# A quarter of the expert tables leaves the gathers: 4,096 of 16,384 experts computed densely on TensorE in a product-key expert FFN

## The reference, cut to what matters

```python
q  = (ht @ w_q).reshape(T, 8, 2, 128)            # 8 heads, two half queries
v1, i1 = top_k(q[:, :, 0] . sub_k1, 16)          # 128 sub keys each
v2, i2 = top_k(q[:, :, 1] . sub_k2, 16)
sc, ci = top_k(v1[..., :, None] + v2[..., None, :], 16)
eidx = e1 * 128 + e2                             # e1, e2: the sub keys; 16384 experts
gate = softmax(sc)
a    = einsum('cd,chkd->chk', h, u_emb[eidx])    # 8 * 16 experts for each token
out  = einsum('chk,chkd->cd', gate * gelu(a), v_emb[eidx])
hs   = rms_norm(hs + out)                        # meta tokens dropped
```

## Time and profile before

| | us |
|---|---|
| median of 3 runs (2062.25 to 2065.85) | 2062.91 |
| the profiled execution | 2061.19 |
| its span on the core | 2059.4 |
| PE busy in the span | 1281.3 |
| DVE busy | 1206.6 |
| POOL busy | 730.3 |
| ACT busy | 410.8 |
| moved by DMA | 686.92 MB, 334 GB/s mean |

### The profile page before, as it was taken

How to read it: one execution, slowest core, us unless ns; L and a number is a source line. 1 busy time by engine, 2 the same in 40 slices (tenths; PEclk the granted TensorE clock), 3 DMA queues, 4 the chain that set the end, 5 groups by cost and what they waited for, 6 DMA issues and landing times.

```text
span 2059.4 us, 21129 instructions
## 1 busy us (share of the span) xinstructions
PE 1281.3 (62%) x7844; PEld 774.2 (38%) x7844; DVE 1206.6 (59%) x2252; ACT 410.8 (20%) x808; POOL 730.3 (35%) x712
## 2 busy tenths in 40 slices
...
GB/s 184 167 172 184 162 200 210 217 190 234 184 184 271 211 353 278 381 421 421 411 421 421 407 421 421 422 421 422 422 421 422 422 422 421 422 421 421 422 408 327
DMA packets 116645, 686.92 MB, mean 334 GB/s; under 512 B 13120, under 2 KB 13120, under 8 KB 42048
## 3 DMA queue, kind: packets, MB, share of 16 engines
q0 software_dynamic: 96768, 589.34, 75.6%
q1 hardware_dynamic: 19792, 96.46, 13.5%
...
## 4 chain that ended last, share of the span: by engine, by line
DMA 49%; PE 34%; DVE 9%; issue 4%; POOL 2%; ACT 1%; DVEq 0%; POOLq 0%; ACTq 0%; SPq 0%
DMA uv<-v_tab,eidT 32%; DMA uv<-u_tab,eid 15%; DVE uv L1473 5%; PE ps L1933 5%; PE ps L1597 4%; PE ps L1514 2%; PE ps L1515 2%; PE ps L1516 2%; PE ps L1602 2%; DMA parts<-W 2%; PE ps L1604 2%; PE ps L1603 2%; POOL uv L538 2%; PE ps L1806 1%; PE ps L1808 1%
## 5 line engine op out<-in xcount | busy, mean ns | idle before, releaser
L1933 PE MATMUL ps<-uv,over_mL 128*32 128x512 f32 x2048 | 459.1, 990 | 726.6 <-DMA uv<-v_tab,eidT 609.7
L1473 DVE CUSTOM_DVE_ANT_0 uv<-uv,xn 128x2048 f32<-128x2048 f32 x256 | 586.3, 2292 | 485.1 <-DMA uv<-u_tab,eid 484.2
L1933 PEld LDWEIGHTS ps<-uv,over_mL 128*32 128x32 f32 x2048 | 51.1, 136 | 1109.9 <-DMA uv<-v_tab,eidT 969.1
L529 POOL DMA_INDIRECT uv<-u_tab,eid x256 | 265.8, 1038 | 567.4 <-DVE av L1473 417.9
L538 POOL DMA_INDIRECT uv<-v_tab,eidT x256 | 285.7, 1116 | 314.1 <-PE ps L1933 295.1
L867 ACT ACTIVATE ga<-av,st 128x16 f32<-128x16 f32 x16 | 4.9, 308 | 724.0 <-DVE av L1473 724.0
L943 DVE TENSOR_TENSOR low_ring<-ring,wh 128x2048 fp32r<-128x2048 f32 x43 | 101.1, 2353 | 74.7 <-ACT wh L569 74.6
L1602 PE MATMUL ps<-hH,parts 128*128 128x256 f32 x400 | 123.8, 309 | 2.0 <-DMA parts<-W 2.0
L501 POOL DMA_DIRECT2D parts<-W x80 | 70.1, 876 | 153.1 <-ACT parts L687 124.6
L1597 PE MATMUL ps<-xn,ring 128*128 128x256 f32 x480 | 113.1, 386 | 0.2
L1895 PE MATMUL ps<-h2T,ring 128*128 128x256 f32 x416 | 112.7, 434 | 0.0
...
## 6 DMA issues: line engine op xcount, KB each, us to landing
...
parts<-W POOLq DMA_DIRECT2D x160, 320.0 KB, 5.5
...
uv<-u_tab,eid POOLq DMA_INDIRECT x256, 17.3
uv<-v_tab,eidT POOLq DMA_INDIRECT x256, 17.6
...
```

The source lines that it names most:

```text
L529: pool.indirect_dma_start(uv[:, m % UV, 0, :], None, u_tab, bass.IndirectOffsetOnAxis(ap=eid[:, p, i:i + 1], axis=0)).then_inc(s_u[m % UV] ...
L1473: nc.vector.tensor_tensor_reduce(uv[:, m % UV, 0, :], uv[:, m % UV, 0, :], xn[:, T, :], 1.0, 0.0, ALU.mult, ALU.add, av[:, p % 2, i:i + 1] ...
L1933: ins = nc.tensor.matmul(ps[32 * n:32 * n + 32, 4 * T + j, :], zd[:, p % 2, 32 * r:32 * r + 32], uv[:, m % UV, 1, n * 512:(n + 1) * 512], ...
```

## The change

`XT` = 32: experts with e1 from 96 to 127 (`E0` = 96) are no longer gathered. Both indirect DMAs get `bounds_check=E0 * NK - 1, oob_is_err=False`, which leaves out the rows with a larger index; the first four v gathers keep the old bound, so that each slot holds finite numbers. `weights` sets the weights of those picks to zero.

For the 4,096 experts left out, all 256 tokens are computed. SP reads `u_tab` in 32 tiles of 128 rows and `v_tab` in 32 tiles of 4 x 128 rows x 512 columns (1 MB each) into `ring`. Per u tile PE makes 16 transposes and 16 matmuls, in four rounds, one behind each pick from 32 on (`dense_inputs`; the first 8 rounds stand ahead of pick 32); ACT copies the transposes (`turned_rows`). DVE scales the products (`act_scaled`), ACT applies gelu. From step `PACK` = 156 the gates are spread over the experts: DVE makes two one-hot tables for 8 tokens at a time (`one_hots`, 32 chunks, three in four steps), PE multiplies them (`gates_spread`), and DVE multiplies the result into the activations (`act_weighted`, 16 times). From step 202 to 265 PE multiplies with the v tiles (`dense_outputs`), four matmuls of 128x512 behind each pick. At step 268 `assembled` brings T = 0 together, and `residual(1, j)` comes at step 271 instead of 128. Both halves now accumulate in banks 0 to 3; ACT copies the first half out at step 160 (`half_kept`). `final(0)` moves to the end. All later queries stand ahead of pick 32.

```diff
@@ POOL: input_rows_of / output_rows_of
                 pool.indirect_dma_start(uv[:, m % UV, 0, :], None, u_tab,
-                                        bass.IndirectOffsetOnAxis(ap=eid[:, p, i:i + 1], axis=0)).then_inc(s_u[m % UV], 16)
+                                        bass.IndirectOffsetOnAxis(ap=eid[:, p, i:i + 1], axis=0),
+                                        bounds_check=E0 * NK - 1, oob_is_err=False).then_inc(s_u[m % UV], 16)
...
+                last = (E0 if m >= UV else NK) * NK - 1
@@ SP
+            for i in range(XT):
+                if i < 2:
+                    sp.wait_ge(s_wdone, RING + W_PQ + 16)
+                else:
+                    sp.wait_ge(s_dt, 4 * (i - 2) + 4)
+                sp.dma_start(ring[:, i % 2, :], u_tab[(E0 + i) * NK:(E0 + i + 1) * NK, :]).then_inc(s_w[i % 2], 16)
+            for k in range(XT):
+                n, m = k // SEG, k % SEG
+                if k < RING:
+                    sp.wait_ge(s_dm, 4 * XT)
+                else:
+                    sp.wait_ge(s_dvd, k - RING + 1)
+                rows4 = slice((E0 + 4 * m) * NK, (E0 + 4 * m + 4) * NK)
+                sp.dma_start(ring[:, k % RING, :].rearrange("p (i c) -> p i c", i=4),
+                             v_tab[rows4, 512 * n:512 * (n + 1)].rearrange("(i p) c -> p i c", p=P)).then_inc(s_w[k % RING], 16)
@@ DVE: weights
+                nc.vector.tensor_scalar(kept[:, :], eid[:, p, :], float(E0 * NK), None, ALU.is_lt).then_inc(s_wp, 1)
+                nc.vector.memset(wp[:, s, :], 0.0).then_inc(s_wp, 1)
                 dve.wait_ge(s_gl, 2 * p + 2)
-                nc.vector.tensor_tensor(wp[:, s, :], ga[:, s, :], gw[:, p, :], ALU.mult).then_inc(s_wp, 1)
+                nc.vector.tensor_tensor(wm[:, :], ga[:, s, :], gw[:, p, :], ALU.mult).then_inc(s_wp, 1)
...
+                nc.vector.copy_predicated(wp[:, s, :], kept[:, :], wm[:, :]).then_inc(s_wp, 1)
@@ DVE: one_hots(c), act_weighted(b)
+                nc.vector.tensor_tensor(oh1[:, c % 2], iota[:, E0:NK].rearrange("p (o n) -> p o n", o=1).broadcast_to([P, 8, XT]),
+                                        over_keys(0, XT), ALU.is_equal).then_inc(s_oh, 1)
+                nc.vector.tensor_tensor(oh2[:, c % 2], iota[:, 0:NK].rearrange("p (o n) -> p o n", o=1).broadcast_to([P, 8, NK]),
+                                        over_keys(1, NK), ALU.is_equal).then_inc(s_oh, 1)
+                dve.wait_ge(s_oh, 3 * c + 1)
+                nc.vector.tensor_tensor(oh1[:, c % 2], oh1[:, c % 2], over_keys(2, XT), ALU.mult).then_inc(s_oh, 1)
...
+                for k in range(XT // SEG):
+                    to = acts[k][:, :, 16 * b:16 * b + 16]
+                    ins = nc.vector.tensor_tensor(to, to, got[:, SEG * k:SEG * (k + 1), :], ALU.mult)
@@ PE: dense_inputs, round n (i, c = n // 4, n % 4)
+                        for k in range(4 * c, 4 * c + 4):
+                            ins = nc.tensor.transpose(ps[:, 4 + n % 2, k % 4 * P:(k % 4 + 1) * P], ring[:, i % 2, k * P:(k + 1) * P], ident)
...
+                        for k in range(4 * c, 4 * c + 4):
+                            ins = nc.tensor.matmul(ps[:, 6 + (i - 1) % 2, 0:SEQ], ring[:, 2 + (i - 1) % 2, k * P:(k + 1) * P], h2T[:, k, :],
@@ PE: dense_outputs
+                        for i in range(4):
+                            for T in range(TT):
+                                ins = nc.tensor.matmul(ps[:, 4 + 2 * (n % 2) + T, :], act_tile(4 * m + i)[:, T * P:(T + 1) * P], v4[:, i, :],
+                                                       start=(m == 0 and i == 0), stop=(m == SEG - 1 and i == 3))
```

More of the change, by code:

```diff
@@ L67 @@
 ZW = 8 * 129
+XT = 32
+E0 = NK - XT
+SEG = 8
 PART = (KT - WHOLE) // 2
@@ L891, in _ @@
             peer_scores(1, 0)
-            for p in range(PAIRS):
+            act.wait_ge(s_tot, 1)
+            nc.scalar.activation(scales, ps[:, 4, SEQ:2 * SEQ], ACT.Copy).then_inc(s_ag, 1)
+            peer_query(0, 1)
+            peer_query(1, 1)
+            gate_exp(1)
+            peer_query(2, 1)
+            peer_scores(0, 1)
+            peer_query(3, 1)
+            peer_query(0, 2)
+            peer_scores(1, 1)
+            gate_exp(2)
+            peer_query(1, 2)
+            gelus(0, 0)
@@ L893, in _ @@
+            peer_query(2, 2)
+            peer_scores(0, 2)
+            peer_query(3, 2)
+            gate_exp(3)
+            peer_query(0, 3)
+            peer_scores(1, 2)
+            peer_query(1, 3)
+            peer_query(2, 3)
+            peer_scores(0, 3)
+            gate_exp(4)
+            peer_query(3, 3)
+            peer_scores(1, 3)
+            for n in range(EARLY_ROUNDS):
+                turned_rows(n)
+            for p in range(1, PAIRS + 1):
                 exps = list(chosen_in(p)) if p < PH // 2 else []
@@ L894, in _ @@
                 for i in range(PICKS):
-                    if p and i == 1:
+                    at = PICKS * p + i
+                    if i == 0:
                         gelus(p - 1, 1)
+                        if p == PAIRS // 2 + 1:
+                            half_kept(0)
+                    for n in rounds_at(at):
+                        turned_rows(n)
+                        if n % (4 * SEG) == 8 and n > 4 * SEG:
+                            act_gelu(n // (4 * SEG) - 1)
                     if i % 8 == 5 and i // 8 < len(exps):
@@ L1466, in _ @@
                     "p (o c) -> p o c", o=1).broadcast_to([32, 4, 32])).then_inc(s_sums, 1)
-            for p in range(PAIRS):
+            nc.vector.memset(ones, 1.0).then_inc(s_sums, 1)
+            for T in range(TT):
+                nc.vector.tensor_scalar(roots_on[:, T, :], ident, st[:, 2 + T:3 + T], None, ALU.mult).then_inc(s_sums, 1)
+            for p in range(PAIRS + 1):
                 T = p // 4
```

288 lines of the change are left out of this document (233 added, 55 removed).

## The result

The changed kernel takes **2037.99 us** (median of 4 runs, 2035.95 to 2041.24), the kernel before 2062.58 us (4 runs, 2061.53 to 2065.85). The ratio is 0.988, 95% interval [0.9862, 0.9897]. It is faster by 24.6 us, 1.2% (the scatter of its own runs is 5 us); I had forecast 64. The profiled execution took 2037.88 us, its span is 2036.1 us.

What follows compares the result with a forecast made beforehand. The DMA engines were taken to bound the expert stage. Stages of 837 + 551 + 207 + 277 put dot 256 at 1872; with 5 + 47 + 49 + 12 + 10 the span is 1995, the forecast 1999 us, range 1948 to 2078.

Steps and rivals of the forecast that it cites:

- the rate of 0.3105 us a row: Expert stage: DMA time per 8 KB row and engine, from 16 rows each in a 4.97 us period.
- would only draw level: Steps 156 to 201: PE needs 2.3 us per pick, 4.6 at the low clock, against DVE's 4.5.
- Bytes alone: Whole expert stage: 1081 rows per engine go, 512 come for tables; net 569 rows x 0.3105 = 177 us.
- Steps 32 to 155, 551 us: These 124 picks: DMA sets the pace with 1773 rows, 4.44 us per pick, PE and DVE fitting under it.
- The term for unevenness: Kept rows in steps 32 to 155: the busiest DMA engine has 5% more than the mean of 1460.
- Steps 156 to 201, 207 us: These 46 picks: DVE becomes the bound at 4.5 us per pick, above DMA's 4.1.
- Steps 202 to 255, 5.13: These 54 picks: DMA takes 892 rows, 277 us, 5.13 per pick; PE's 4.7 is covered.
- Rival C: Steps 202 to 265: PE's clock stays near 0.8, so PE sets 5.9 us per pick; 2053 us, chance 0.13.
- The end, 128 us from dot 255: After the u picks: 47 us of dense outputs, 49 for steps 266 to 287, 12 at the end.
- Rival A: All DMA engines wait for the slowest at each turn of the slots, +13% instead of +5%; 2070 us, chance 0.14.
- rival B: DMA engines stay balanced or drift is free, and seams are hidden; 1950 us, chance 0.13.
- Rival D: A skipped row is not free; at a full row's price steps 156 to 201 take 229 us; 2230 in all, chance 0.08.

Runs made afterwards that it cites:

- e6: The changed kernel without the bound check, so all rows are gathered and the dense work is still done: 2228.94 us, 1.0806 of before.
- e1: The kernel before with only the bound check added on both gathers, without the dense work: 1870.23 us, 0.9066 of before.
- e5: The changed kernel with experts' numbers altered so each gather skips exactly one of each four neighbouring partitions' rows: 2020.54 us, 0.9796 of before.
- experiment 5: Follow-up on steps 156 to 201 of the changed kernel, 4.98 us a step; its waits read: who waited <- for whom: us in all, times, longest.
- e4: The changed kernel with three of four matmuls that spread the gates left out: 2012.37 us, 0.9755 of before.
- e7: The changed kernel with the two one-hot tables in fp32r, one record per spread matmul instead of two: 2010.41 us, 0.9743 of before.
- e11: The changed kernel with the gate-spreading matmul's operands exchanged, 32 columns loaded and 128 streamed: 2009.80 us, 0.9745 of before.

## Why the prediction was half right

The direction and the mechanism held: rows that are skipped cost almost nothing, the tables cost their bytes, and DMA stays the bound but for one stage. The size did not: 25 us instead of 64. Two steps of the sum failed: the rate of 0.3105 us a row in steps 32 to 155, and the sentence that PE at the low clock "would only draw level" in steps 156 to 201. By the steps of the prediction:

- **Bytes alone, 177 us.** Both sides of this account were measured apart. The tables: 159 forecast, 166 measured (e6). The skip: 1081 rows x 0.3105 = 336 us in my account; 193 in the kernel before (e1), and 191 beside the dense work (2228.9 - 2038.0). My stages had already left part of it out, since the start and the stages of other bounds don't gain. That 193 and 191 agree is chance: in steps 156 to 201 the skip gives 37 us in the kernel before and 12 beside the dense work, and in the steps 32 to 155 and 202 to 254 together 147 and 178.
- **Start, 837:** 838.4. The twelve queries were hidden.
- **Steps 32 to 155, 551 us: 575.** The term for unevenness was right as a sum. e5 is 15.0 us shorter over these steps, and has 12 rows where the real choice has 11.78 in the mean, which is another 124 x 0.22 x 0.317 = 9 us: 24 together, where +5% of 1460 rows made 23. It isn't spread as I had it; all that evenness visibly gave came in steps 64 to 127 (what it gave in steps 32 to 63 is hidden behind the longer wait of e5, up to 6 us). What failed is **the rate of 0.3105 us a row**, read from one pick. With even rows, e5, the whole stretch takes 559.7 us for 124 x 12 rows and 28 table tiles (the trace has 28 issued there, not 30), 1712 rows: 0.327 us a row. At that rate my sum with 28 tiles, 1757 rows, gives 574.5, the measured time; at 0.3105 it gives 546, so that 29 us are the rate's. Two parts of it, 21 us, can be named. First, a row costs 0.314 to 0.318 in steps 96 to 127 of the changed kernel, what a skipped one leaves included: some 11 us on 1773 rows. Second, the kernel before itself needs 5.06 us a step over steps 32 to 254, not 4.97: (1964.94 - 837.16) / 223, from the earlier trace rows. 11 us of that excess lie in steps 32 to 63 (5.32), and the changed kernel has 10 there. I took the period of the calm part for all. In both, POOL waits there once for the experts' numbers (before, then after; form as in experiment 5):

```profile
POOL uv L529 <- DVE eid L1412: 12.9, 1, 12.9
```

```profile
POOL uv L599 <- DVE eid L1541: 10.7, 1, 10.7
```

  That this wait makes the excess was not tested. The 6 us gained in steps 128 to 155 are no merit of the sum: only four table tiles are issued there, against eight in each 32 steps before, while I had spread them evenly.
- **Steps 156 to 201, 207 us: 229.** The sizes were right: PE 4.6 us at the low clock by my sum, 4.50 to 4.65 measured, and DVE 4.5, with 4.4 measured once it sets the pace. The step that failed is the sentence that PE's 4.6 "would only draw level". It lies above DVE's 4.5 already, so PE becomes the bound, and PE's own waits for DVE, which I had put at nothing, add 0.5 us a step: 4.98. With PE's load or its low clock taken away (e4, e7, e11) the stage falls to 4.4, so this step is shown. I had priced the clock as a rival only for the steps 202 to 265, and against it I had said that PE comes up whenever it is busy without a gap; from 1460 to 1480 us of after it was busy 20.00 of 20 us, and the granted clock stayed at 0.50.
- **Steps 202 to 255, 5.13: 5.17**, with PE busy 200.64 of 222 us at a clock of 1.00. Rival C is out in its place, though its mechanism is what happened one stage earlier.
- **The end, 128 us from dot 255: 119.6.** The 10 us for seams stand in this sum; the rest of it, 118, was nearly right. From PE's timeline:

```profile
1966.84 3.70 PE L2196 MATMUL ps<-ring,sct 128*128 128x512 f32 x8
1970.47 2.78 PE L2122 MATMUL ps<-uv,late 128*32 128x512 f32 x24
1973.07 1.04 PE L2208 MATMUL ps<-xn,prm 128*32 128x512 f32 x8
...
1983.95 3.62 PE L2060 MATMUL ps<-hs,prm 128*32 128x512 f32 x32
1987.38 1.04 PE L2122 MATMUL ps<-uv,late 128*32 128x512 f32 x8
...
2023.83 1.93 PE L2122 MATMUL ps<-uv,late 128*32 128x512 f32 x8 [2.93 <-DMA uv<-v_tab,eidT]
```

  A dense step is 4.62 us (1962.22 to 1966.84 in the same view; 4.7 forecast), `assembled` 8.3 (7.7), the residual 3.4 (4.0), and the last pick stands 12.3 us before the end (12). The last sixteen picks take 36 us from the first's start to the last's (1987.38 to 2023.83) instead of 28: DMA is at 0.75 there, and most picks wait for a landing. The three picks ahead of `assembled` and the steps 255 to 265 took less than forecast. The 10 us for seams are not to be seen in one place.
- **Rival A** (all wait for the slowest, +13%) and **rival B** (balanced) are both out: +5% is what even rows and their count say. The map of partitions to engines that the Trainium skill gives ("DMA: Bandwidth & Descriptors", The descriptor swizzle) led to +4.6% over these steps, and the measured 24 us of 453 are +5.3%. That rows made even by groups of 8 partitions took the loss away agrees with it; a choice that is even in another grouping was not run.
- **Rival D** (a skipped row at full price) is out by e1. Its sum also left out the four v tiles of steps 156 to 201: with them these are 238 us, not 229.
